# Expert bodies regrouped in a two-layer diffusion block: two 32-token experts in the large body, a 64-token expert in the 128-token body

## The reference, cut to what matters

```python
def swiglu(h, wg, wu, wd):
    return (jax.nn.silu(h @ wg) * (h @ wu)) @ wd

def moe_ffn(h, w_router, b_router, wg, wu, wd):
    logits = (t @ w_router).astype(jnp.float32) + b_router.astype(jnp.float32)
    top_v, top_i = lax.top_k(logits, TOP_K)
    w = jax.nn.softmax(top_v, axis=-1)
    combine = jnp.sum(jax.nn.one_hot(top_i, N_EXPERTS, dtype=jnp.float32) * w[..., None], axis=1)
    for e in range(N_EXPERTS):
        out = out + combine[:, e:e + 1] * swiglu(t, wg[e], wu[e], wd[e])
```

## Time and profile before

| | us |
|---|---|
| median of 3 runs | 2213.91 |
| the runs | 2212.33, 2213.91, 2215.14 |
| span of the profiled execution | 2215.4 |
| TensorE busy (matmul) | 2026.0, 91% of the span |
| VectorE, ScalarE, POOL busy | 994.7, 753.7, 580.3 |
| moved by DMA | 514.91 MB |

### The profile page before, as it was taken

The page is one execution under the profiler, slowest core; times in us unless marked ns, Lnnn a source line. Parts: engine busy times, 40 slices in busy tenths (PEclk is TensorE's granted clock), DMA queues, the critical chain, the costliest instruction groups (busy, mean ns, idle before and its releaser), DMA issues.

```text
span 2215.4 us, 34627 instructions
## 1 busy us (share of the span) xinstructions
PE 2026.0 (91%) x13806; PEld 1437.5 (65%) x13806; DVE 994.7 (45%) x1471; ACT 753.7 (34%) x1005; POOL 580.3 (26%) x350
## 2 busy tenths in 40 slices
PE   6999799997999999989888599999999999988886
PEld 3655477777877878845677466666566656666664
DVE  5345521386222336755425643333454333455555
ACT  3146622244121234235432232323332323234442
POOL 0112412260122134112334023333213312123431
PEclk8999999998999999999999699999999999999997
DMA  7311034451444445411365369999989999979993
GB/s 285 100 43 39 20 114 152 173 196 49 147 158 152 152 144 197 132 43 39 114 229 171 153 252 375 401 395 417 389 324 373 420 419 421 419 310 409 419 421 132
DMA packets 158819, 514.91 MB, mean 232 GB/s; under 512 B 8492, under 2 KB 72108, under 8 KB 115524
## 3 DMA queue, kind: packets, MB, share of 16 engines
q1 hardware_dynamic: 158660, 512.69, 60.7%
HBM read 511.61 MB, written 1.05 MB: 231 GB/s over the span
## 4 chain that ended last, share of the span: by engine, by line
PE 67%; issue 9%; DVE 8%; DMA 7%; POOL 5%; ACT 3%; SPq 0%; DVEq 0%; ACTq 0%; POOLq 0%
PE psum L862 65%; DMA e_more<-in_experts 3%; POOL w_lo L2887 3%; DMA e_ring<-in_experts 1%; DVE w_lo L2158 1%; ACT w_hi L1684 1%; PE psum L1140 1%; DMA ring<-in_w_out 1%; DVE reg_q L2372 1%; DMA ring<-in_w_mod 1%; DMA ring<-in_w_in 1%; DVE stat L2379 1%; POOL p_last L2864 0%; PE psum L1574 0%; POOL h_t L2872 0%
## 5 line engine op out<-in xcount | busy, mean ns | idle before, releaser
L2839 POOL TENSOR_TENSOR w_lo<-ring,w_hi 128x512 fp32r<-128x512 f32 (+1 forms) x92 | 208.8, 2272 | 598.8 <-ACT w_hi L1684 598.6
L2887 POOL TENSOR_TENSOR w_lo<-e_ring,w_hi 128x512 fp32r<-128x512 f32 x92 | 205.6, 2236 | 536.3 <-PE psum L862 292.9
L2158 DVE TENSOR_TENSOR w_lo<-ring,w_hi 128x1536 fp32r<-128x1536 f32 (+1 forms) x92 | 171.1, 1866 | 328.2 <-ACT w_hi L1684 328.1
L862 PE MATMUL psum<-e_ring,reg_q 128*32 128x128 f32 (+3 forms) x4664 | 279.3, 319 | 11.6 <-DVE reg_q L2744 3.1
L1684 ACT ACTIVATE w_hi<-ring 128x2048 fp32r<-128x2048 f32 (+1 forms) x92 | 167.7, 1830 | 341.8 <-DMA ring<-in_w_in 81.5
L2057 ACT ACTIVATE w_hi<-e_ring 128x2048 fp32r<-128x2048 f32 x92 | 175.8, 1912 | 222.4 <-DMA e_ring<-in_experts 215.1
L862 PEld LDWEIGHTS psum<-e_ring,reg_q 128*32 128x32 f32 (+1 forms) x4664 | 175.3, 117 | 106.7 <-issue 58.2
L2158 DVE TENSOR_TENSOR w_lo<-e_ring,w_hi 128x1536 fp32r<-128x1536 f32 x92 | 177.0, 1928 | 135.3 <-PE psum L862 89.2
L862 PE MATMUL psum<-h_hi,w_hi 128*128 128x512 f32 (+1 forms) x400 | 150.3, 376 | 11.8 <-issue 9.5
L862 PE MATMUL psum<-h_lo,w_hi 128*128 128x512 f32 (+1 forms) x400 | 147.9, 370 | 0.0
L862 PE MATMUL psum<-h_hi,w_lo 128*128 128x512 f32 (+1 forms) x400 | 147.7, 369 | 0.0
(11 more groups left out here) (327 smaller groups left out, 3807.9 us busy)
## 6 DMA issues: line engine op xcount, KB each, us to landing
e_ring<-in_experts SPq DMA_DIRECT2D x240, 1024.0 KB, 10.4
e_more<-in_experts SPq DMA_DIRECT2D x96, 1024.0 KB, 10.6
ring<-in_w_mod SPq DMA_DIRECT2D x48, 1024.0 KB, 7.9
ring<-in_w_in SPq DMA_DIRECT2D x22, 1024.0 KB, 5.3
ring<-in_w_ff_down SPq DMA_DIRECT2D x22, 1024.0 KB, 5.0
ring<-in_w_out SPq DMA_DIRECT2D x12, 1024.0 KB, 5.8
ring<-in_w_ff_gate SPq DMA_DIRECT2D x11, 1024.0 KB, 5.3
ring<-in_w_ff_up SPq DMA_DIRECT2D x11, 1024.0 KB, 5.4
```

What stands on the lines that cost most here:

```text
L862: ins = pe.matmul(o, lhs, rhs, start=start, stop=stop, **kw)
L2158: return dve.tensor_tensor(dst, src, hi.bitcast(F32), ALU.subtract)
L2839: pool.tensor_tensor(w_lo[:, n % SLOTS, a:size], ring[:, n % SLOTS, a:size], w_hi[:, q % HIS, a:size].bitcast(F32), ALU.subtract).then_inc ...
L2887: pool.tensor_tensor(lo_slot[slot][:, LO_DVE:SLOT], e_slot[slot][:, LO_DVE:SLOT], w_hi[:, (n_split + t) % HIS, LO_DVE:SLOT].bitcast(F32), ...
```

## The change

The large body takes two 32-token experts `a` and `b`, the middle body a 64-token `a` and a 32-token `b` as before, and the 128-token body a 64-token `b`. The order of the light blocks keeps its pattern, with `a` for `h` and `b` for `q`. All light outputs now lie as 128 x 512 in two halves of 64 rows: a 32-token expert sums in a separate 128 x 256 tile `y_part` and is put into that layout by the last multiplication with the gate, four instructions of 32 rows. `spread` is then one matmul of 64 rows by 512 columns for each part, and `b`'s parts are issued in pairs. The weight of a `b` expert is copied to `b_w` at `select` (step 30). SP gets a loop of its own for the middle body, since the light slots of the two kinds of body are counted differently. Cut to its core (names `h` and `q` replaced by `a` and `b` throughout):

```diff
-LIGHT = {"h": P // 2, "q": P // 4}
-HALVES = {c: P // m for c, m in LIGHT.items()}
+FEW = {True: {"a": P // 4, "b": P // 4}, MID: {"a": P // 2, "b": P // 4}, False: {"b": P // 2}}
+LIGHT = ("a", "b")
...
-BLOCKS = {True: block_order("hhqhqhqhqhhqqq"), False: block_order("q" * NFC)}
+BLOCKS = {True: block_order("aabababab" + "aabbb"), False: block_order("b" * NFC)}
...
-        def light_at(two, c, g, twos, total):
-            return total + g if c == "h" else total + twos + g
+        def light_at(two, c, g, wides, twos, total):
+            if FEW[two][c] == SECOND:
+                return total + g - wides
+            return total + total - wides + g + (twos if c == "a" else 0)
...
-            with sp.Fori(0, twos) as g:
-                pair_body(True, g, twos, total)
+            wides, mids = heavy_counts(sp)
+            with sp.Fori(0, wides) as g:
+                pair_body(True, g, wides, twos, total)
+            with sp.Fori(0, mids) as i:
+                pair_body(MID, sp.snap(i + wides), wides, twos, total)
...
-            def spread(c, n, banks):
+            def spread(c, n, bank):
                 t, dh = divmod(n, 2)
-                m = LIGHT[c]
-                for i, bank in enumerate(banks):
-                    at = len(banks) * dh + i
-                    rows = slice(at * m, (at + 1) * m)
-                    mm(psum[:, bank, 0:512 // len(banks)], sel_slot_l[c][rows, t, :], y_l[c][rows, :],
-                       start=True, stop=True, sig=l_sc_mm[c] if i == len(banks) - 1 else None)
+                rows = slice(dh * SECOND, (dh + 1) * SECOND)
+                mm(psum[:, bank, :], sel_slot_l[c][rows, t, :], y_l[c][rows, :], start=True, stop=True, sig=l_sc_mm[c])
...
                 def light(c, kind, b):
-                    m = LIGHT[c]
-                    tiles = HALVES[c]
+                    m = FEW[two][c]
+                    tiles = P // m
...
+                        if c == "b":
+                            spread(c, n, 5)
+                            spread(c, n + 1, 6)
...
             for n in range(4):
                 scatter(n, (6, 7, 4, 5)[n], False)
-                if n >= 2:
-                    pe.wait_ge(l_sc_ok["q"], total * 4 + n - 1)
-                spread("q", n, (2, 3) if n % 2 == 0 else (0, 1))
+                spread("b", n, (2, 3, 0, 1)[n])
...
+            dve.tensor_tensor(over[:, 2:3], over[:, 2:3], n_jobs[:, 2:3], ALU.add)
...
-            link(dve.tensor_scalar(steps, e_num, 2.0, need[:, 2:3], ALU.mult, ALU.is_lt))
-            link(dve.reduce_sum(need[:, 2:3], steps, AX.X))
+            dve.tensor_scalar(steps[:, 0, :], e_num, 2.0, need[:, 1:2], ALU.mult, ALU.is_lt)
+            link(dve.tensor_scalar(steps[:, 1, :], e_num, 2.0, need[:, 2:3], ALU.mult, ALU.is_lt))
+            link(dve.reduce_sum(need[:, 1:3], steps, AX.X))
...
                     elif op == "select":
                         select(two, g + 1)
+                        dve.wait_ge(l_sc_ok["b"], g * 4 + 4)
+                        dve.tensor_copy(b_w, job_w[:, :, bass.ds(slot_at(slot_l["b"] + 1, NSLOT), 1)]
+                                        .rearrange("p t s -> p (t s)")).then_inc(b_w_ok, 1)
...
                         if b == NFC - 1:
-                            ins = dve.tensor_tensor(y_l[c], y_l[c], gate_l[c], ALU.mult)
+                            if m == SECOND:
+                                ins = dve.tensor_tensor(acc, acc, gate_l[m], ALU.mult)
+                            else:
+                                for q in range(P // m):
+                                    rows = slice(q * m, (q + 1) * m)
+                                    ins = dve.tensor_tensor(y_l[c][rows, q % 2 * cols:(q % 2 + 1) * cols], acc[rows, :],
+                                                            gate_l[m][rows, :], ALU.mult)
```

More of the change, by code:

```diff
@@ L159, in light @@
         put(down, ("ldown", c, b))
-    first = "h" if two else "q"
+    first = "a" if two else "b"
     put(0, ("gather", first))
@@ L165, in expert_plan @@
     for n in range(4):
-        put(n + 4 if two else 2 + n // 2, ("spread", "q", n))
+        put(n + 4 if two else 2 + n // 2, ("spread", "b", n))
     put(8, ("turn_sel",))
@@ L177, in expert_plan @@
     if two:
[L178 to L181, removed]
+        put(33, ("spread", "a", 0))
+        amid[34].append(("spread", "a", 1))
+        put(34, ("spread", "a", 2))
+        amid[35].append(("spread", "a", 3))
     for fc in range(NFC):
@@ L522, in build @@
         at[0] = 8192
-        gate_l = {"h": part(512), "q": part(256)}
+        gate_l = {P // 2: part(512), P // 4: part(256)}
+        x_l["b"] = part(KD * SECOND).rearrange("p (k n) -> p k n", k=KD)
+        y_part = {c: part(256) for c in LIGHT}
         route_c = part(R_END)
@@ L564, in build @@
         need = rpart(4)
-        steps = rpart(NE)
+        steps = rpart(2 * NE).rearrange("p (a e) -> p a e", a=2)
+        b_w = rpart(2)
         n_jobs = rpart(4)
         n_jobs_i = rpart(4).bitcast(I32)
-        assert rt_at[0] <= 1484
+        assert rt_at[0] <= 1496
         def job_counts(eng):
@@ L812, in _, with pair_body @@
                 load(n)
-            def pair_body(two, g, twos, total):
+            def pair_body(two, g, wides, twos, total):
                 base, _ = in_body(sp, two, g, twos)
-                at = {"e": g, **{c: slot_at(light_at(two, c, g, twos, total)) for c in (("h", "q") if two else ("q",))}}
+                at = {"e": g, **{c: slot_at(sp.snap(light_at(two, c, g, wides, twos, total))) for c in FEW[two]}}
                 src = {c: w["experts"][bass.ds(sp.value_load(job_ei[0:1, bass.ds(s, 1)], min_val=0, max_val=NE - 1), 1)]
@@ L1556, in pair_body @@
                         pe.wait_ge(l_a_ok[c], j7 + (b + 1))
-                        for i in range(512 // HALVES[c] // P):
+                        for i in range(4 * FEW[two][c] // P):
                             ins = pe.transpose(psum[:, 7, i * P:(i + 1) * P], l_a[:, i * P:(i + 1) * P], ident)
@@ L2017, in _ @@
             act.wait_ge(mod_done, mod_at[(1, 11)] + 1)
-            for c in LIGHT:
-                m, wide = LIGHT[c], D // HALVES[c]
-                for i in range(HALVES[c]):
-                    ins = act.activation(gate_l[c][i * m:(i + 1) * m, :],
+            for m in gate_l:
+                wide = D * m // P
+                for i in range(P // m):
+                    ins = act.activation(gate_l[m][i * m:(i + 1) * m, :],
                                          gate2[i * m:(i + 1) * m, 1, i * wide:(i + 1) * wide], ACT.Copy)
@@ L2091, in pair_body @@
                         _, c, b = step
-                        wide = 512 // HALVES[c]
+                        wide = 4 * FEW[two][c]
                         act.wait_ge(w_used, used(two, base, c, "up", b))
```

154 lines of the change are left out of this document (83 added, 71 removed).

## The result

The changed kernel takes 2205.98 us (median of 20 runs, 2197.59 to 2213.84) against 2215.22 us for the kernel before on the same chip (20 runs): a ratio of 0.9963, 95% interval 0.9952 to 0.9974, that is -8.2 us (the two medians alone differ by 9.2). The direction was forecast, the size was not: -19 us was expected. The profiled execution took 2206.64 us with a span of 2204.8 us, 10.6 less than the span of before.

The account below looks back on a forecast made before the run. The bound was taken to change hands: TensorE in the large body, DMAs in the rest of the middle and 128-token bodies. -24 - 1 + 6.7 - 0.5 = -19 us from 2213.9 gave 2195 us, range 2181 to 2211.

Parts of the forecast that it names:

- the standstill left at the end of the large body: Large body's rest: of 15 us without chunk movement, 1 to 2 stay for end lumps such as the gather; 14 gained.
- the start of the 128-token body: First block's gate and up, four wider chunks at 0.82 us, +3.3, less 1 for a VectorE wait: +2.3 us.
- its end: 128-token body's end: last block's down pair adds 1.6 us, the 5.2 us wait for VectorE shrinks by 3: -1.4.
- the waits for VectorE in the middle body: Middle body: `b` outputs put back by one 64x512 matmul, in pairs, so one wait falls away: -1 us.
- the tail: Final scatter: one matmul for two of the same columns and two waits fewer, -0.5 us, bound 0 to -1.
- rival (b): Large body already at the DMA wall; only the start's 10 us come: -5 us in all, 2209 us, chance 0.15.
- Large body, -24: Large body: start 10 us shorter from two narrower blocks, rest 14 us shorter as the DMAs become the bound.
- the boundary was therefore worth nothing: Middle body's start: its 14 us standstill isn't from TensorE arriving late, so entering it DMA-bound gains nothing.
- 128-token body, +6.7: 128-token body: start +2.3, rest +5.8 from cycles of 30.8 us, end +1.6 and -3; bounds +1 to +15.
- rival (a): 128-token body hides nearly all its new work: +1 there, -25 in the large body, 2188 us, chance 0.20.
- rival (c): 128-token body's idle time is its own chain's latency, so all 35 us show: +9.5, 2223 us, chance 0.08.
- 3 steps or more before anything reads it and hidden by TensorE's heavy parts: Last gate product as four VectorE instructions, some 1.2 us more, claimed to cost nothing because of this cover.

Follow-up runs that it names:

- one product: Changed kernel with the last gate product as one 128x512 VectorE instruction in place of four of 32 rows: 2203.18 us, 0.9947 against the kernel before.
- six slots: Changed kernel with 6 slots in place of 7 in the 128-token body's chunk ring: 2212.79 us in its one run.
- pairs in the tail: Changed kernel with the final spreads after the last body issued in pairs: 2204.43 us, 0.9962 against the kernel before.
- other order: Changed kernel with the middle body's light blocks reordered, 32-token blocks first: 2195.47 us, 0.9928 against the kernel before.
- large body undone: Changed kernel with the large body's `a` at 64 tokens again, 128-token body and layout as changed: 2221.31 us, 1.004 against the kernel before.
- the layout alone: Changed kernel with the old expert grouping (64 + 32 in the large body, 32 in the 128-token body): 2220.02 us, 1.002 against the kernel before.
- the narrow expert: Changed kernel with the 128-token body's light expert computed for 32 tokens only, leaving out its tokens beyond: 2198.5 us, 0.993 against the kernel before.
- all three with one product: The one-instruction gate kernel, and two adding paired final spreads and a new middle-body block order, each a different order: 2203.18, 2195.69, 2194.28 us.

## Why the prediction was half right

The forecast was -19 us and -8.2 were measured. The steps that failed are four terms of the sum: the standstill left at the end of the large body (1 to 2 us, measured 3 to 6), the start of the 128-token body (+2.3, measured +5.5) with its end (-1.4, measured about 0), the waits for VectorE in the middle body (-1, measured +0.8) and the tail (-0.5, measured +1.6).

**What bounds the kernel: right.** The bound changes hands between the bodies, and TensorE work moved from the first to the last as the busy times said: a block's 5.0 us gave -10.3 us in the large body's start, and the width cost the last body 10.6 us with its clock. That rules out rival (b): the large body's rest gave 9 to 12 us and so had not stood at the wall of the DMAs, and the clock there stayed at 0.99 with TensorE 94% busy. (One reading was wrong: "99% of both stretches" holds for the rest alone; in the start it is 63.73 of 65.40 us, 97%.)

**Large body, -24 against -21.** The term that failed is "of the 15 us of standstill I leave 1 to 2 for the lumps at the end". Cut by steps, here of the kernel before,

```profile
1347.20:1581.00 233.80, 233.25 (x1996) 144.21 (x1995) 84.97 (x98) 68.82 (x66) 75.24 (x30) 1.00 0.98 399
1581.00:1629.10 48.10, 46.39 (x516) 31.54 (x514) 19.67 (x34) 15.81 (x23) 14.77 (x6) 1.00 0.85 339
```

the standstill was 12 us in steps 7 to 35 and 9 in steps 36 to 41. The first part is what can be won, and was (9 to 12). The second lies in steps where TensorE is the bound with work that the change doesn't touch, and it stayed: 48.1 us before and after. My window ended inside those steps (at 1617.1 of 1629.1), and so made one number of two causes. With 14 us forecast for the rest and 9 to 12 won, the lump and what else is left above the floor cost 3 to 6 us of the 15, not 1 to 2.

**Middle body, -1 against 0 to +1.** The wait for VectorE that falls away is within what the profiles scatter: the same middle body took 331.5 to 333.4 us in seven profiles, against 332.4 and 332.5 before. One part is steady: the start, steps 0 to 6, took 64.8 us in each of the seven and 64.1 in both of before. TensorE waits 0.16 us for the light selection in front of the light gather there, where it had not waited, and 0.4 of the 0.7 us have come by the end of that gather; with one product the start takes 64.4. So the four products cost here too, where the forecast hid them. That its start stays TensorE-bound whatever the stretch before it was right; that the boundary was therefore worth nothing was right of this change only.

**128-token body, +6.7 against +11.6.** Its rest was right to the microsecond: a cycle of 30.9 us for 30.8, and steps 3 to 37 179.1 us for 173.4, +5.7 where +5.8 stood. So rival (a) falls, which had it all hidden, and rival (c), which needed cycles of 34 us; yet (c) named a real resource, since one slot less costs 1.9 us a cycle. (Its chain was read too long: VectorE takes 1536 columns of a chunk and POOL the other 512, and both wait for ScalarE, not for each other.) Two other terms failed. The first is the start, +2.3 against +5.5. The light pairs cost about what was said (29.1 us in the kernel with one product, at the clock of 0.94 that before had at 26.7). The four products were priced rightly, at +1.2 for 1.28, but "3 steps or more before anything reads it and hidden by TensorE's heavy parts" looked only for the reader of the product. What it delays is the next instruction on VectorE, the light selection for the next body, for which TensorE waits in the first step. The largest piece is half clock: the changed kernel ran 10.2 us at half clock there in both of its profiles, with a gather of 6.67 us for 3.76 before, and four kernels with the same code in this body's start and the same wait of 1.6 us (pairs in the tail, other order, six slots, large body undone) ran it at full clock in 28.7 us, 3.5 less. Steps 0 to 2 of before, of the changed kernel and of the one with the other order:

```profile
1961.50:1988.20 26.70, 24.12 (x218) 17.06 (x217) 16.27 (x29) 7.74 (x8) 6.27 (x4) 0.94 0.69 278
```

```profile
1938.30:1970.50 32.20, 30.58 (x150) 21.01 (x149) 17.34 (x31) 7.63 (x8) 4.78 (x4) 0.84 0.59 234
```

```profile
1927.40:1956.10 28.70, 25.89 (x149) 16.75 (x148) 18.09 (x31) 7.58 (x8) 4.88 (x4) 1.00 0.65 265
```

(The pieces don't add up to 5.5 exactly, as each kernel had its own share of half clock.) The two kernels with a 32-token expert there have the same wait, and 10.2 us (the layout alone) and 6.8 us (the narrow expert) at half clock; with the short wait it is 3.4 us, in both profiles of before and in all three with one product. So the wait alone doesn't bring the clock down, and what does stays open. As long as it is open, the forecast could not have had the 3.5 us: the wait it could have had. The second term is the end, -1.4 against 0: the wait of 5.2 us did shrink by 2.9, where I had said 3, but TensorE was busy 2.3 us longer for 1.6 and waited 0.5 us longer for the last low part.

**Tail, -0.5 against +1.6.** "One matmul for two of the same columns" had the sign wrong: the two had run at the same time, and VectorE waits for the first two parts. The row that would have told was the earlier trace rows, where four records of 32x256 take 0.70 us; the count of matmuls isn't their time.

Together: 3 us in the large body, 2 in the middle, 5 in the last and 2 in the tail are missing from the forecast, 12 us, and turn -19 into -7, which is what the lengths give and near the -8.2 us of the ratio.

## What to carry to other kernels

Before moving work from a stretch where an engine is the bound to one where it is idle, cut the stretch by the program's own steps and subtract the other resource's floor in each; only a standstill in steps that lose work is won. Order inside a body can be worth as much as regrouping between bodies: look which parts lie in the stretch with no slack, and put the heavy optional ones elsewhere. And of an instruction that gets longer, ask what stands behind it in its queue, not only who reads its output.

## What was not expected of the hardware

- Two float32 matmuls on different row groups ran fully side by side (two 64x512 in 2.08 us against one in 2.07 at half clock, 1.13 against 1.12 at full clock), so a "merge" of two narrow matmuls into one of twice the columns made the spread slower by 0.85 us.
- At one place the granted clock was at half level for 10.2 us in both profiles of one kernel and at full level all through in four profiles of kernels with the same code there and the same wait before it; it was worth 3.5 us. Neither of the two kernels that were profiled twice differed between its profiles.
- The start of the expert stage, which the change hardly touches, moved by 8 us between profiles (1269.4 to 1277.3), as much as the whole effect.
